# Four pairs of the second block's weights, issued behind the last gather

## The reference

```python
def peer(h, w_q, subkeys, u, v):
    ...
        q = (xc @ w_q).reshape(C, PEER_HEADS, 2, PEER_HALF)
        s = jnp.einsum('chpd,hpnd->chpn', q, subkeys)
        sv, si = lax.top_k(s, PEER_TOPK)
        ...
        ids = jnp.take_along_axis(cand_id..., pos, axis=-1)      # 8 heads x 16 experts a token
        g = jax.nn.softmax(best, axis=-1)
        ue = jnp.take(u, ids, axis=0)
        ve = jnp.take(v, ids, axis=0)
        a = jax.nn.gelu(jnp.einsum('cd,chkd->chk', xc, ue))
        return jnp.einsum('chk,chkd->cd', g * a, ve)

x = first_block(...)           # attention, then x + g2x * peer(...), then a norm
h = rms_norm(x, norm_mix_g)    # second block
proj = h @ w_in                # eight groups of columns: ca, cg, q, f, i, g, gc, gr
...                            # convolution and gated recurrence, cross attention on mem, mixture of experts
```

## Time and profile before

| | |
|---|---|
| median of 3 runs | 1747.97 us (1747.78 to 1748.62) |
| the profiled execution, its own time | 1741.25 us |
| its span, first to last instruction | 1739.5 us |
| TensorE (matmuls) busy | 1446.3 us, 83% |
| VectorE busy | 895.4 us, 51% |
| ScalarE busy | 561.8 us, 32% |
| POOL busy | 294.6 us, 17% |
| DMA | 571.89 MB, mean 329 GB/s |
| granted TensorE clock, mean | 0.927 of 2.4 GHz |

### The profile page before, as it was taken

One profiled execution on the slowest core, in us unless ns is written; L12 is line 12 of the kernel. 1 busy time (PEld: TensorE's weight loads), 2 busy tenths in 40 slices (PEclk: granted clock), 3 DMA queues, 4 the chain that ended last, 5 costly groups with the idle time before them and its releaser, 6 DMA issues.

```text
span 1739.5 us, 21127 instructions
## 1 busy us (share of the span) xinstructions
PE 1446.3 (83%) x7808; PEld 881.0 (51%) x7808; DVE 895.4 (51%) x2104; ACT 561.8 (32%) x1402; POOL 294.6 (17%) x277
## 2 busy tenths in 40 slices
PE   5999876877886767666656999999989999999997
PEld 4586743534542223333112899887744454544343
DVE  4787577476666666666765887522131212111112
ACT  3113467354544444444444146302121111111111
POOL 0100033233344444434441000000000000000000
PEclk8999988889989787788788999999999999999999
DMA  9771179899999999999995534453489999999994
GB/s 396 273 268 61 37 298 368 328 426 399 378 413 427 424 421 426 422 427 426 416 427 218 204 125 146 155 185 111 178 339 427 428 428 427 427 427 428 428 427 181
DMA packets 80002, 571.89 MB, mean 329 GB/s; under 512 B 9137, under 2 KB 9393, under 8 KB 11185
## 3 DMA queue, kind: packets, MB, share of 16 engines
q1 hardware_dynamic: 40608, 284.55, 40.2%
q0 software_dynamic: 39312, 286.28, 40.1%
HBM read 569.75 MB, written 1.05 MB: 328 GB/s over the span
## 4 chain that ended last, share of the span: by engine, by line
PE 53%; DMA 26%; DVE 13%; ACT 4%; issue 2%; POOL 1%; SPq 0%; DVEq 0%; POOLq 0%; ACTq 0%
DMA big<-in_peer_dram,misc 15%; PE bank L1689 12%; DMA big<-in_moe_down_dram 10%; PE bank L1496 8%; PE bank L1337 7%; DVE big L2000 5%; PE bank L1134 4%; PE bank L1282 2%; PE bank L1138 2%; PE bank L1677 2%; PE bank L1564 2%; DMA ring<-in_first_dram 1%; PE bank L1359 1%; POOL big L620 1%; PE bank L1248 1%
## 5 line engine op out<-in xcount | busy, mean ns | idle before, releaser
L1337 PE MATMUL bank<-big 128*64 128x512 f32 x1024 | 311.3, 740 | 184.6 <-ACT big L796 183.1
L620 POOL DMA_INDIRECT big<-in_peer_dram,misc x256 | 285.2, 1114 | 522.8 <-PE bank L1337 366.4
L1337 PEld LDWEIGHTS bank<-big 128*64 128x64 f32 x1024 | 72.6, 158 | 361.9 <-ACT big L796 248.8
L2000 DVE SCALAR_TENSOR_TENSOR big<-big 128x1024 f32<-128x1024 f32 x128 | 155.8, 1224 | 109.4 <-DMA big<-in_peer_dram,misc 108.6
L2000 DVE SCALAR_TENSOR_TENSOR big<-big,misc 128x1024 f32<-128x1024 f32 x128 | 154.5, 1222 | 84.1 <-DMA big<-in_peer_dram,misc 83.7
L1689 PE MATMUL bank<-big 128*64 128x512 f32 x640 | 140.3, 592 | 1.3 <-ACT big L1019 1.3
L790 ACT ACTIVATE misc<-misc 128x1 f32<-128x1 f32 x256 | 51.4, 201 | 273.7 <-DVE big L2000 261.2
L1689 PE MATMUL bank<-big,misc 128*64 128x512 f32 x512 | 114.9, 596 | 19.5 <-DMA big<-in_moe_down_dram 13.4
L1496 PE MATMUL bank<-H,ring 128*128 128x256 f32 x448 | 102.3, 391 | 5.9 <-DVE H L2095 3.0
L1496 PEld LDWEIGHTS bank<-H,ring 128*128 128x128 f32 x448 | 87.9, 197 | 19.8 <-issue 7.2
L1689 PEld LDWEIGHTS bank<-big 128*64 128x64 f32 x640 | 50.7, 137 | 87.4 <-issue 85.7
(11 more groups left out here) (409 smaller groups left out, 2266.3 us busy)
## 6 DMA issues: line engine op xcount, KB each, us to landing
big<-in_moe_down_dram SPq DMA_DIRECT2D x64, 1024.0 KB, 20.0
ring<-in_second_dram SPq DMA_DIRECT2D x36, 1024.0 KB
ring<-in_first_dram SPq DMA_DIRECT2D x33, 1024.0 KB
big<-in_moe_gate_dram SPq DMA_DIRECT2D x32, 1024.0 KB, 20.4
big<-in_moe_up_dram SPq DMA_DIRECT2D x32, 1024.0 KB, 19.3
ring<-in_moe_gate_dram SPq DMA_DIRECT2D x32, 1024.0 KB, 22.2
misc<-in_mod_rest_dram POOLq DMA_DIRECT2D x16, 1024.0 KB, 6.0
big<-in_moe_far_up_dram SPq DMA_DIRECT2D x16, 1024.0 KB, 23.9
```

The source lines that it names most:

```text
L620: pool.indirect_dma_start(out=gathered[b % GATHERS], out_offset=None, in_=t["peer"], in_offset=bass.IndirectOffsetOnAxis(ap=rows[:, b % 32 ...
L1337: last = nc.tensor.matmul(bank[2 * tt + half][HALF * g:HALF * (g + 1), :], diag[:, b % DIAGS, :], gathered[b % GATHERS][:, a:a + 512], sta ...
L2000: dve.scalar_tensor_tensor(u, u, 1.0, x_pairs[b // (BLOCKS // 2)][:, b % 2, :], ALU.mult, ALU.mult, accum_out=dots[:, b % 32:b % 32 + 1]). ...
```

## The change

One wait is put into SyncE's program, ahead of the loop that issues the first four pairs of `SECOND`:

```diff
             def load_second(m):
                 load_pair(PAIRS1 + m, t["second"][m])
 
+            sp.wait_ge(S(f"gathered{(BLOCKS - 1) % GATHERS}"), 16 * ((BLOCKS - 1) // GATHERS + 1))
             for m in range(RING):
                 first_done(sp, *FIRST[2 * (PAIRS1 - RING + m) + 1])
                 load_second(m)
```

## The result

| | before | changed |
|---|---|---|
| median | 1747.78 us (5 runs, 1742.45 to 1748.62) | 1732.29 us (5 runs, 1728.25 to 1739.86) |
| profiled execution, own time / span | 1741.25 / 1739.5 us | 1728.25 / 1726.4 us |
| ratio, changed to before | | 0.9922, 95% interval 0.9893 to 0.9951 |

The changed kernel is faster, by 0.5 to 1.1%. The forecast was a gain of 9.6 us (a ratio of 0.9945, inside the interval), 1738.4 us in a range of 1737.0 to 1742.2; the measured median lies 4.7 us under the range. So the way was right, and the number wasn't. A ratio of 0.9922 is a gain of 13.6 us (the two medians by themselves are 15.5 apart). The question for the experiments is whether four loads are worth 13.6 us, or 9.6 with something else beside them.

The account below looks back on a forecast made before the run. DMA transfers were taken to bound gather stages 9 to 14. Four loads removed, −9.8 us, plus 0.2 lost behind them, gave −9.6 us from the timed median 1747.97: 1738.4 us, range 1737.0 to 1742.2.

Parts of the forecast that it names:

- What bounds stages 9 to 12: Gather stages 9 to 12: DMA transfers set the pace, at a share of 1.00 to 1.02; removing four loads saves 9.8 us.
- The term: Each 1024 KB load taken out of the gathers saves its bytes' time at 426 GB/s, 2.46 us.
- The estimate from the Trainium skill: The four loads costed at the page's HBM limit of about 358 GB/s: 11.7 us, result near 1736.3 us.
- What is lost behind it, 0.2 us: In the gathers, removed loads no longer hide moments when the gathers' own queue is short: 0.2 us lost.
- the window of 367 GB/s at 711.61: A 2.5 us traffic drop in the gathers, taken as the hole left by a gather issued only 6.93 us ahead.
- The bound of 3.6 us: Most that could be lost: 2.8 us for holes behind eight value products plus 0.8 for one slow issue.
- The loads behind the last gather cost nothing: After block 255 lands, the four loads fit into 13.92 us of empty DMA engines, hidden by the chain: cost nothing.
- The 6.0 us taken for a first load from the earlier trace: Issue to landing of one 1024 KB transfer on a quiet core, leaving the first pair some 7.9 us early.
- That VectorE, POOL or the value products take the pace: Rival in stages 9 to 12: consumers set the pace, half the gain left, 4.9 us, 1743.1 us; chance 0.06.
- That loads issued early are free: Rival: loads fall in holes of the gathers' queue, so nothing is gained, 1748.0 us; chance 0.04.
- TensorE's clock behind them: Rival at the second block's products: late pairs lower TensorE's clock, 13.9 us slower, 1752.3 us; chance 0.02.
- The signs: Expected profile: stages 9 to 12 at 39.4 to 40.1 us, last dot product about 927.6, then 13.9 us to the first product.

Follow-up runs that it names:

- the third profile of the changed kernel: The changed kernel timed and profiled once more, no edit, against the kernel before: ratio 0.9939; 279.20 us from stage 9 to the last dot product.
- the run with two loads: Against the kernel before, the wait put between the second and third load, so two stay in stages 9 and 10: ratio 0.9972.
- this case's 49.04 against 39.24 us: Against the kernel before, the wait set for block 208, so all four loads go out in stage 13: ratio 0.9993.
- a real wait of 4.9 us: Against the kernel before, the loads wait for the first eighth of the second block's scaled input, when they are wanted: ratio 0.9983.

## Why the prediction was right and wrong

**What bounds stages 9 to 12: right.** They are bound by bytes. With four loads between stage 9 and the last dot product it takes 285.3 us (mean of three profiles), with two 279.6, with none 276.0 (mean of seven): 2.3 us a load, or 2.5 without the third profile of the changed kernel and its dips. The term was 2.46. The estimate from the Trainium skill ("DMA: Bandwidth & Descriptors", Specifications, about 358 GB/s from HBM for a core), 11.7 us, gave a time nearer to the measured median, but by accident: every whole stage above shows 415 to 427 GB/s.

**What is lost behind it, 0.2 us: near enough in size, wrong in reading.** In the changed kernel stages 10 and 11, with their value products, take 39.25 and 39.24 us, 0.05 over 16 × 2.45; nothing was lost in them. Stages 9 and 12 took more, 40.07 and 41.09, but such excess is there with the loads too. At 2.45 us a gather the 111 from the start of stage 9 to the last dot product would take 272.0 us. The seven profiles without a load lie 4.0 us over that in the mean, and the three with four loads lie 3.5 over that and 9.8. So 0.5 us is what was lost by these means, with single profiles up to 4 us apart: these runs can't tell it from 0.2 or from nothing. But the window of 367 GB/s at 711.61, which I read as a hole in the gathers' queue, has 14% fewer bytes at a share only 5% lower, so 10% more engine time for each byte. By these numbers it was mostly one of the dips above. The bound of 3.6 us that I made from it had the wrong cause.

**The loads behind the last gather cost nothing: right.** The first product waits for the norm. The 6.0 us taken for a first load from the earlier trace rows was high, it is 4.85 to 4.94; the chain over the norm covers it with 9 us to spare, and 4.2 us of them can be given away.

**The rivals.** That VectorE, POOL or the value products take the pace: no, by the stages at 39.25 and by the run with two loads. That loads issued early are free: no. Issued early, in stages 9 to 13, these four cost 9.8 us; issued late, nothing. The rule of the Trainium skill ("DMA: Bandwidth & Descriptors", Rules for kernel authors) is to issue early and wait late, and what it says is hidden by that is the fixed setup cost; the prediction took it for the time of the bytes too, and this case's 49.04 against 39.24 us show that this isn't so where the engines are full. TensorE's clock behind them: no, 0.97 and 1.00 in the products, and 0.96 and 0.97 behind a real wait of 4.9 us.

**The signs.** Of what the prediction said the profile would show, three things missed, and no run ties any of them to the change. The last dot product came at 923.7 and not 927.6, 3.9 us early, and 3.4 of them were there when stage 9 started. One of stages 9 to 12 was over the 41 us that it had called a sign of being wrong (41.09; the four in the mean, 39.91, were within 39.4 to 40.1). In the two profiles of the kernel before, these stages differ as much among themselves (41.8 to 43.4 us). And the stretch before the first product took 15.5 us at 0.89 and not 13.9, while the products behind it took 55.5 us at 1.00 and not 57.1 within 0.5. The sign named for it was that the clock falls under 0.9 in that product's stretch; it fell as low in the kernel before against itself (0.80), with no load there.

**The step that failed** is in how the numbers follow: "half the spread of the timed runs (1747.78 to 1748.62, so 0.4)". Three runs that agree within 0.84 us were taken for the spread of the kernel. Its timings go from 1738.7 to 1754.1 over 67 runs, and the changed kernel's from 1728.3 to 1739.9 over 17; the medians of five stand with an interval of 0.3% either way, 5 us. The profiled execution had said so: it took 1741.25 us where the three took 1748, and I noted the 6.7 us and gave them no place in the range. The gain forecast for the change, 9.6 us, is inside the intervals of all three measurements, and of the 10.6 ± 1.8 over all runs. The 6.1 us by which the result lies under the forecast come apart like this: 3.0 because 1747.97 was above the kernel's mean of 1744.9, 1.0 because the gain is 10.6 and not 9.6 (a difference that these runs can't tell from nothing), 2.1 because the median of the changed kernel's first five runs was under its own mean of 1734.4. That the three runs under the forecast came out high and the five of the result low is chance. With 5 us in the place of the 0.4 the range would have begun at 1747.97 − 10.5 − 5 = 1732.5, still 0.2 above the result. The 0.2%, 3.5 us, given as what a measurement can tell from no change was too small in the same way: five runs gave 0.3%.

**Still open:** what sets the clock of the first 40 us and the length of the stages ahead of stage 9, which spread 11 us over the profiles of programs that are the same up to there; and what the loads cost beyond the 4.9 us of waiting when they are issued only as they are wanted. No run here takes them apart.

## What to carry to other kernels

Where the DMA engines are full, a load costs the time of its bytes (here in stages 9 to 12 as in stage 13), so look for a stretch in which they are empty and move loads there that are not wanted before: 2.46 us each for 1024 KB at 426 GB/s. Check the cover by the chain (here 13.9 us against 4.9 for the first load), and issue in the order of need. Before giving a range for a gain of half a per cent, look at how far the profiled execution stands from the timed ones: three timings close together say little.

## What the runs showed of the hardware

Three things that I had not expected. The DMA engines have dips of some microseconds in which they are nearly as busy as ever (a share of 0.95 to 1.04 in the windows shown) and move 315 to 400 GB/s instead of 427; over the seven profiles without loads in it the stretch from stage 9 to the last dot product varies from 274.7 to 279.2 us, and the longest has the most dips. TensorE's granted clock in a stretch differs between executions of one program: 0.81 to 0.91 in the first 40 us, in which all eleven profiles run the same program, and 0.99 and 0.80 behind the gathers in the two profiles of the kernel before, which there makes 13.9 and 17.3 us of the same work. The mean clock alone doesn't give the time (15.7 us came with 0.78): what counts is which instructions the low stretches fall on. And a load of 1024 KB on empty engines takes 4.9 us until the waiting product may start, 0.94 of it before the first packet moves.
